# A hybrid attention layer on one core: first weight quarter on ScalarE's queue, and x's tile 0 turned once

## The reference, cut to what matters

```python
ms = jnp.mean(xf * xf, axis=-1, keepdims=True)
h = xf * lax.rsqrt(ms + eps) * g            # rmsnorm(x, norm_pre_g)
u = jnp.einsum('bsd,de->bse', h, w_in)      # x: (1, 512, 1024), w_in: (1024, 4096)
```

## Time and profile before

| | us |
|---|---|
| median of 3 runs | 254.0 (253.83 to 255.63) |
| the profiled execution | 254.23 |
| its span, first to last instruction | 252.4 |
| TensorE busy | 245.6 |
| VectorE busy | 177.0 |
| ScalarE busy | 143.0 |
| GpSimd busy | 32.7 |

### The profile page before, as it was taken

How to read it: one execution, slowest core, us unless ns; L and a number is a source line. 1 busy time by engine, 2 the same in 40 slices (tenths; PEclk the granted TensorE clock), 3 DMA queues, 4 the chain that set the end, 5 groups by cost and what they waited for, 6 DMA issues and landing times.

```text
span 252.4 us, 4450 instructions
## 1 busy us (share of the span) xinstructions
PE 245.6 (97%) x1567; PEld 123.2 (49%) x1567; DVE 177.0 (70%) x393; ACT 143.0 (57%) x336; POOL 32.7 (13%) x74
## 2 busy tenths in 40 slices
PE   8999999999999999999999999999999999999991
PEld 6454444445444554544455444454444444555570
DVE  2998585587478688868877767977787896835313
ACT  4777565375356666574677595667565665611110
POOL 1329300000000320041031033000000000111101
PEclk9999999999999999999999999999999999999998
DMA  6978979605656545544935644568849869982422
GB/s 242 366 245 173 310 251 371 218 28 135 106 160 163 180 114 130 140 163 112 203 103 136 137 161 119 136 189 184 174 103 201 209 157 170 202 203 43 125 86 83
DMA packets 59674, 42.47 MB, mean 168 GB/s; under 512 B 45808, under 2 KB 46072, under 8 KB 59652
## 3 DMA queue, kind: packets, MB, share of 16 engines
q1 hardware_dynamic: 59636, 42.18, 63.5%
q10 hardware_dynamic: 16, 0.00, 0.0%
HBM read 29.04 MB, written 2.13 MB: 123 GB/s over the span
## 4 chain that ended last, share of the span: by engine, by line
PE 97%; DVE 1%; DVEq 0%; POOLq 0%; issue 0%; ACT 0%; POOL 0%; ACTq 0%
PE unit_ps L578 72%; PE score_ps L634 6%; PE o_ps L655 5%; PE unit_ps L608 4%; PE unit_ps L589 3%; PE unit_ps L615 2%; PE unit_ps L543 1%; PE score_ps L536 1%; PE score_ps L709 1%; PE unit_ps L709 1%; DVE area L1058 0%; DVE gates L956 0%; DVEq L180 0%; POOLq L180 0%; ACT junk L732 0%
## 5 line engine op out<-in xcount | busy, mean ns | idle before, releaser
L578 PE MATMUL unit_ps<-area,w_hi 128*128 128x512 f16 x256 | 76.2, 379 | 0.0
L788 ACT ACTIVATE arena<-arena,negmax 128x512 f32<-128x512 f32 (+3 forms) x64 | 35.4, 554 | 49.5 <-DVE negmax L985 49.4
L578 PE MATMUL unit_ps<-w_hi,area 128*128 128x512 f16 x192 | 60.3, 379 | 0.0
L578 PE MATMUL unit_ps<-area,w_lo 128*128 128x512 f16 x128 | 48.5, 379 | 0.0
L578 PEld LDWEIGHTS unit_ps<-area,w_hi 128*128 128x128 f16 x256 | 24.1, 98 | 27.2 <-issue 1.1
L578 PE MATMUL unit_ps<-w_lo,area 128*128 128x512 f16 x96 | 36.4, 379 | 0.0
L985 DVE CUSTOM_DVE_ANT_0 arena<-score_ps,strips 128x512 f32<-128x512 f32 (+3 forms) x64 | 28.6, 485 | 9.2 <-PE score_ps L634 9.2
L882 DVE SCALAR_TENSOR_TENSOR w_lo<-stage,g_cols,w_hi 128x512 f16<-128x512 f32 x32 | 24.2, 755 | 11.3 <-ACT w_hi L746 11.2
L578 PEld LDWEIGHTS unit_ps<-w_hi,area 128*128 128x128 f16 x192 | 18.8, 98 | 21.9 <-DVE w_lo L888 0.7
L745 ACT ACTIVATE w_hi<-stage,g_cols 128x512 f16<-128x512 f32 x32 | 22.7, 711 | 7.3 <-DMA stage<-in_w_in_dram 7.3
L884 DVE SCALAR_TENSOR_TENSOR w_lo<-stage,g_cols,w_hi 128x512 f16<-128x512 f32 x32 | 24.8, 777 | 0.0
(11 more groups left out here) (106 smaller groups left out, 357.7 us busy)
## 6 DMA issues: line engine op xcount, KB each, us to landing
stage<-in_w_in_dram SPq DMA_DIRECT2D x32, 512.0 KB, 4.3
stage<-in_w_out_dram SPq DMA_DIRECT2D x8, 512.0 KB, 4.2
arena<-in_x_dram SPq DMA_DIRECT2D x4, 512.0 KB, 5.2
strips<-bias_rows SPq DMA_DIRECT2D x4, 512.0 KB, 4.7
stage<-in_x_dram SPq DMA_DIRECT2D x4, 512.0 KB, 4.7
out_dram<-area SPq DMA_DIRECT2D x3, 512.0 KB, 2.7
strips<-bias_rows SPq DMA_DIRECT2D x1, 1024.0 KB, 7.8
pt<-arena SPq DMA_TRANSPOSE x32, 3.1
```

The costliest lines, as they stand in the source:

```text
L578: last = nc.tensor.matmul(bank, a, b, start=(k == 0 and n == 0), stop=(k == KT - 1 and n == 2))
L788: nc.scalar.activation(probs[:, i % 2, m, 0:n], probs[:, i % 2, m, 0:n], ACT.Exp, bias=negmax[:, i, m:m + 1], scale=-1.0, accum_out=sums[: ...
```

## The change

The first issue of ScalarE's queue becomes the load of w0, and SyncE's queue loses it. The load of g moves from ScalarE's queue to GpSimd's, ahead of the building of the identity. The second turn of x0 and the scaling of its rows (`x_norm(0)`) go. In their place VectorE multiplies a 128 by 128 tile of ones by the row factor of each row (`repeat_factor`); TensorE turns that tile once, behind the turn of x1, into `o_ps`; VectorE copies it out and multiplies the raw turned x0, which still stands in PSUM, by it (`x_scale`), between its part of unit 0 and the lower half of x3 (`xn_lo(3)`). The halves of x0 are taken from that product, in SBUF. x1 is turned where it was.

```diff
@@ sync
             load_x(0)
-            load_quarter(0)
             load_quarter(1)
             load_x(1)
@@ gpsimd
+            nc.gpsimd.dma_start(g_rows[:, :], norm_pre_g[0].rearrange("(k p) -> k p", p=P)).then_inc(gpre_loaded, 16)
             nc.gpsimd.memset(ident[:, :], 0.0).then_inc(ident_zero, 1)
@@ tensor
             for q in range(4):
                 first_quarter(q)
-                if q in (0, 2):
-                    t = q // 2
-                    pe.wait_ge(xs_ready, t + 1)
-                    x_transposes(t, range(KT), xt_ready)
+                if q == 2:
+                    pe.wait_ge(xs_ready, 1)
+                    x_transposes(1, range(KT), xt_ready)
+                    pe.wait_ge(factor_ready, 1)
+                    nc.tensor.transpose(o_ps[:, 0, 0:P], factor_rows, ident[:, :]).then_inc(factor_turned, 1)
@@ scalar
             def x_hi(t):
-                act.wait_ge(xt_ready, t + 1)
-                nc.scalar.activation(ht[:, 0, :, t * P:(t + 1) * P], x_columns(t), ACT.Copy).then_inc(ht_hi_ready, 1)
+                if t == 1:
+                    act.wait_ge(xt_ready, 1)
+                    src = x_columns(1)
+                else:
+                    act.wait_ge(x_scaled_ready, 1)
+                    src = x_scaled
+                nc.scalar.activation(ht[:, 0, :, t * P:(t + 1) * P], src, ACT.Copy).then_inc(ht_hi_ready, 1)
...
-            nc.scalar.dma_start(g_rows[:, :], norm_pre_g[0].rearrange("(k p) -> k p", p=P)).then_inc(gpre_loaded, 16)
+            first = GROUPS[0][2]
+            nc.scalar.dma_start(stage[:, 0, :].rearrange("p (k n) -> p k n", k=2),
+                                w_in_v[:, 0:2, first:first + WIDTH]).then_inc(w_loaded[0], 16)
             x_square(0)
@@ vector
+            def repeat_factor():
+
+                dve.wait_ge(x_rstd_ready, 1)
+                dve.wait_ge(warm_ready, 1)
+                nc.vector.tensor_scalar(factor_rows, warm, x_rstd[:, 0:1], 1.0, ALU.mult,
+                                        ALU.mult).then_inc(factor_ready, 1)
+
+            def x_scale():
+
+                dve.wait_ge(factor_turned, 1)
+                nc.vector.tensor_copy(factor_cols, o_ps[:, 0, 0:P]).then_inc(factor_read, 1)
+                dve.wait_ge(factor_read, 1)
+                dve.wait_ge(x_first_turned, 2)
+                dve.wait_ge(x_squared, 1)
+                nc.vector.tensor_tensor(x_scaled, x_columns(0), factor_cols.unsqueeze(1).to_broadcast([P, KT, P]),
+                                        ALU.mult).then_inc(x_scaled_ready, 1)
...
             def x_lo(t):
                 dve.wait_ge(ht_hi_ready, HT_COUNT[t])
                 cols = slice(t * P, (t + 1) * P)
-                nc.vector.tensor_tensor(ht[:, 1, :, cols], x_columns(t), ht[:, 0, :, cols],
+                src = x_columns(1)
+                if t == 0:
+                    dve.wait_ge(x_scaled_ready, 1)
+                    src = x_scaled
+                nc.vector.tensor_tensor(ht[:, 1, :, cols], src, ht[:, 0, :, cols],
                                         ALU.subtract).then_inc(ht_ready, 1)
...
             x_weigh(1)
-            x_norm(0)
+            repeat_factor()
             split(0)
...
             unit(0)
+            x_scale()
             xn_lo(3)
```

More of the change, by code:

```diff
@@ L256, in bass_hymba_diff_moba_layer @@
         warm = gates[:, 1, 2, 0:P]
+        factor_rows = gates[:, 1, 2, P:2 * P]
+        factor_cols = gates[:, 1, 2, 2 * P:3 * P]
+        x_scaled = x_sb[:, 0, :].rearrange("p (k s) -> p k s", s=P)
         x_first = gates[:, 1, 0:2, :].rearrange("p t (k s) -> p (t k) s", s=P)
@@ L317, in bass_hymba_diff_moba_layer @@
         first_read = sem("first_read")
+        factor_ready = sem("factor_ready")
+        factor_turned = sem("factor_turned")
+        factor_read = sem("factor_read")
+        x_scaled_ready = sem("x_scaled_ready")
         xt_ready = sem("xt_ready")
```

## The result

The changed kernel took 257.53 us (median of 6 runs, 256.88 to 258.19) against 254.07 for the kernel before beside it: a ratio of 1.0127, with an interval of 1.0095 to 1.016. The forecast was 254.4, no change, and its range ended at 255.9. The profiled execution took 258.08 us, its span 256.2, which is 3.8 us more than the span of before.

What follows compares the result with a forecast made beforehand. TensorE was taken as the bound, busy 245.6 of 252.4 us. Terms -0.87, +0.87, +0.11 and +0.25 gave +0.36 on 254.23: 254.6 profiled, 254.4 as a median, no measurable change; range 253.4 to 255.9.

Steps and rivals of the forecast that it cites:

- part 3: Start of TensorE's queue: g issued by GpSimd lands at 4.0, covered by x0's own delay; price nothing.
- rival 3: TensorE's start: g landing late delays x0's turn, and slow pace may add; +1 to +2.6 us; chance 0.17.
- Part 2: First loads: x0 lands at 5.05, w0 at 6.9, w2 and x1 unchanged; x0's 0.62 us delay is hidden.
- rival 1: Early loads: w1 and x1, issued 0.46 us sooner, also land sooner; -0.2 us, so 253.8; chance 0.17.
- Part 1: TensorE's early turns: second turn of x0 removed, 0.87 us, factor's turn added, 0.11; the gain goes into waiting for w2.
- the forecast wait for w2: TensorE between quarters 1 and 2: quarter 1 ends at 10.67, then TensorE waits for w2 until 10.98.
- Part 4: VectorE behind unit 0: `x_scale` takes about 1.45 us, 0.96 covered by idle time, so later work moves by 0.45.
- The wait of unit 3 for its bank: TensorE at unit 3: VectorE returns unit 1's bank at 25.87 instead of 25.42, so unit 3 starts 0.36 us later.
- The forecast +0.36: Whole kernel: -0.87 turn, +0.87 waiting for w2, +0.11 factor, +0.25 rest of the bank wait.

Runs made afterwards that it cites:

- the hole filled: The changed kernel with twelve more small matmuls on a constant ahead of g's turn (`WARM_UP` [17, 1, 1] for [5, 1, 1]): 256.73 us, ratio 1.0093 to the kernel before.

## Why the prediction was wrong

**What failed: part 3, g by GpSimd, and with it the chance of rival 3.** The prediction's price for this part was nothing; in the changed kernel TensorE lost 3.45 us waiting for g. The prediction put g's landing at 4.0, with a far bound of 5.3 taken from a 64 KB load. Measured 6.87. Two errors are in it. The step reasoned that "it is 4 KB beside the first bytes", as if a small load were served soon; the runs show that the same 4 KB took longer the more traffic there was beside it: 2.02, 3.10, 4.48 and 5.62 us with 0, 0.5, 2 and 2 MB (the last in two queues). And the issue itself began at 1.24, not near 0.72, when x0's load and w0's had been issued. The far bound was no bound: that 64 KB load was one issue of the same queue, not the third queue's first issue behind two full ones. Rival 3 had the mechanism, the place and the point of decision (about 4.7), and the further cost of the hole: its chance of 0.17 was too low and its top of 256.6 too near. Its own arithmetic with g at 6.87 gives a turn of x0 at about 7.8, and 7.97 was measured. Its quarter 2 at 11.55 for g at 5.3 was summed wrongly: a turn at 6.2, quarter 0 behind it by the 1.88 us of the rows, and two quarters give 11.78.

**The pace after the hole.** Rival 3 allowed 1.7 us for it. The excess of quarters 0 to 2 was 6.50 - 5.16 = 1.34 us in the changed kernel, and in the profiled execution with the hole filled 1.08 of it was gone. How much of that the hole causes stays open, since the rise also moves without it: g moved alone and g behind w0 have the same TensorE queue up to quarter 0 and the same hole, and their rises are at 9.20 and 10.54. The prediction read its windows' 1.00 as the clock of the early work; the trace of the kernel before has no clock record ahead of 5.28, and the half pace that the prediction found ahead of it is the lower level.

**Part 2, the order of the loads, failed in its rule.** "Neither has a lead over the other" gave x0 at 5.05 and w0 at 6.9; it was 4.81 and 5.7. In this order the error was small. But the rule behind it, that loads of two queues share evenly, is not what the runs show: a lead of 0.45 us decided 1.5 us of x0's landing (4.81 or 6.30). That a load is not delivered sooner for being issued from another queue was right: w0, issued 0.46 us sooner, landed at 5.7 as before. The Trainium skill, DMA: Bandwidth & Descriptors, section Issuing engines are not separate DMA queues, says that such loads interleave on the same 16 DMA engines and that only the issue time is saved. The trace agrees on the second for w0; on the first the section gives no shares, and the traces show very uneven ones (0.46 MB against 0.05 from 2 to 4 us). For the loads behind, the forecast that they land where they did was wrong too: w1 landed at 7.1, x1 at 8.4 and w2 at 10.1 in the changed kernel, against 8.2, 9.5 and 10.8 before, which is more than the 0.46 us by which w1 and x1 were issued sooner. That is the condition of rival 1, and g's hole hid what it would have been worth. How much of it is the new order is open, since the run with the single turn and the old loads has x1 at 8.9 and w2 at 10.2.

**Part 1 held, where it could be seen.** With the old loads the single turn left a wait of 0.74 us for w2 in place of the 0.87 us removed, and the time was unchanged. In the changed kernel itself the forecast wait for w2 is absent, since TensorE was by then 3.7 us late and w2 had landed. The factor's turn is 0.11 us, as summed.

**Part 4 held in size and was hidden in the change.** `x_scale` took 1.46 us (forecast 1.45), and put VectorE back by 0.36 in the run with the single turn alone (forecast 0.45). The wait of unit 3 for its bank did not occur in the changed kernel, whose TensorE was later than VectorE; it appeared, with 0.15 us, once the hole was filled. The forecast +0.36 for the time was not met in the run with the single turn alone (0.0 by the medians, within -0.7 to +0.3 by its interval); x1 and w2 landed some 0.65 us sooner in that profiled execution than in the one of before, with the same queue, and how much of the result is due to that stays open.

**The sum as measured.** Quarter 0 is 3.76 us later (3.46 of hole, 0.3 of slower work around it); quarters 0 to 2 with what lies between them took 6.50 instead of 6.58, since the slow pace ate what the second turn gave; the factor's turn adds 0.11. Together 3.79, and 3.77 at unit 4. Set against the run with g alone on GpSimd: 2.23 us are g's new issuer, 1.16 that g landed later still with w0 in ScalarE's queue, 0.11 the factor's turn, and 0.29 that the work from quarter 0 to quarter 2 took 6.50 us against 6.21 there, second turn included.

## What to carry to other kernels

Before a load is moved to another queue, ask what will be in flight at the moment when it is issued there, and what its consumer has queued behind it. A small load that gates everything belongs at the very front of a queue, ahead of the first large load in time, not only on a queue that is empty; and look at what it displaces, since w0 behind g landed at 8.1 here and x0 behind g, with w0 in the lead, at 6.3. And work taken out of the bounding engine gains only up to the next landing of data: look for what is there just in time before counting it. A profile is one execution: see where its time lies among the others before its microseconds are taken for the change's, and don't read a clock column where the trace has no clock record.

## What the runs showed of the hardware that was not expected

A 4 KB load issued by GpSimd took 2.02 us alone and 5.62 us with 2 MB issued around the same time on two other queues. A 512 KB load took 5.0 us when it was issued at the same moment as another (0.73), and 6.8 when it was issued 0.6 us later (w0 at 1.34, landed at 8.10). GpSimd's first DMA issue began at 1.24 and took 0.77 us, where ScalarE and SyncE began at 0.73 and took 0.40 to 0.60. TensorE's first work and its work after a hole ran at half the pace (x0's eight transposes 1.71 us instead of 0.87) until the first clock record, and with the same queue of TensorE that record began at 4.57 in one execution and at 9.61 in another.
